# Attention with sinks: the rotation of keys and queries by block transfers instead of by products

## The reference, cut to what matters

```python
def apply_rope_2(x, cos, sin):
    x1, x2 = jnp.split(x.astype(jnp.float32), 2, axis=-1)
    return jnp.concatenate([x1 * cos - x2 * sin, x2 * cos + x1 * sin], axis=-1)

def swa_sink_mixer(h, positions, w_qkv, q_norm, k_norm, sinks, w_out):
    qkv = h @ w_qkv
    q, k, v = jnp.split(qkv, [1024, 1280], axis=-1)       # 16 heads, 4 heads, 4 heads of 64
    ...
    q = apply_rope_2(rms_norm_2(q, q_norm), cos, sin)
    k = apply_rope_2(rms_norm_2(k, k_norm), cos, sin)
    o = banded_sink_attention(q, k, v, sinks)
    return o.astype(h.dtype) @ w_out
```

## Time and profile before

| | |
|---|---|
| median of 3 runs | 2091.65 us (2090.82 to 2091.75) |
| the profiled execution | 2096.21 us, of which the span of the instructions is 2094.3 us |
| TensorE busy | 2067.1 us, 99% of the span |
| VectorE, ScalarE busy | 1779.1 us (85%), 1400.0 us (67%) |
| mean granted clock of TensorE | 0.995 of full |
| attention with sinks | from about 1771 us to 1850 us of the span |

### The profile page before, as it was taken

One profiled execution on the slowest core, in us unless ns is written; L12 is line 12 of the kernel. 1 busy time (PEld: TensorE's weight loads), 2 busy tenths in 40 slices (PEclk: granted clock), 3 DMA queues, 4 the chain that ended last, 5 costly groups with the idle time before them and its releaser, 6 DMA issues. The chain is left out here.

```text
span 2094.3 us, 27806 instructions
## 1 busy us (share of the span) xinstructions
PE 2067.1 (99%) x10830; PEld 1740.9 (83%) x10830; DVE 1779.1 (85%) x2358; ACT 1400.0 (67%) x1855; POOL 59.6 (3%) x58
## 2 busy tenths in 40 slices
PE   9999999999999999999999999999999999999999
PEld 8878888878888888888888888879988888778887
DVE  6776768789999999999999999988878888788887
ACT  5654547568888888888888888867745446565544
POOL 0011002001000000000000000000000000000000
PEclk9999999999999999999999999999999999999999
DMA  9537764659999999999999999954446555346552
GB/s 312 181 121 271 233 209 151 219 199 395 394 395 395 395 395 383 385 380 386 371 393 374 388 372 378 394 202 141 144 159 227 196 181 149 81 154 222 183 197 102
DMA packets 291275, 565.92 MB, mean 270 GB/s; under 512 B 13596, under 2 KB 120224, under 8 KB 290896
## 3 DMA queue, kind: packets, MB, share of 16 engines
q1 hardware_dynamic: 284480, 537.13, 71.8%
q0 software_dynamic: 5792, 23.78, 3.1%
q10 hardware_dynamic: 864, 3.15, 0.4%
HBM read 555.10 MB, written 12.59 MB: 271 GB/s over the span
## 5 line engine op out<-in xcount | busy, mean ns | idle before, releaser
L505 DVE TENSOR_TENSOR wl<-raw,wh 128x1024 fp32r<-128x1024 f32 x626 | 756.2, 1242 | 99.9 <-ACT wh L497 95.5
L497 ACT ACTIVATE wh<-raw 128x1024 fp32r<-128x1024 f32 x626 | 640.9, 1053 | 154.1 <-PE psum L542 61.7
L505 DVE TENSOR_TENSOR wl<-arena,wh 128x1024 fp32r<-128x1024 f32 x384 | 456.7, 1222 | 37.6 <-ACT wh L497 32.6
L497 ACT ACTIVATE wh<-arena 128x1024 fp32r<-128x1024 f32 x384 | 403.9, 1062 | 84.7 <-PE psum L542 82.5
L540 PE MATMUL psum<-wh,xhl 128*128 128x512 f32 (+1 forms) x1136 | 449.5, 396 | 1.8 <-DVE wl L505 0.9
L542 PE MATMUL psum<-wh,xhl 128*128 128x512 f32 (+1 forms) x1136 | 441.5, 389 | 0.0
L541 PE MATMUL psum<-wl,xhl 128*128 128x512 f32 (+1 forms) x1136 | 440.6, 388 | 0.0
L532 PE MATMUL psum<-xhl,wh 128*128 128x512 f32 x980 | 349.4, 396 | 0.0
L540 PE MATMUL psum<-wh,yh 128*128 128x512 f32 x752 | 295.6, 393 | 1.0 <-DVE yl L1714 1.0
L542 PE MATMUL psum<-wh,yl 128*128 128x512 f32 x752 | 293.0, 390 | 0.0
L541 PE MATMUL psum<-wl,yh 128*128 128x512 f32 x752 | 292.6, 389 | 0.0
(11 more groups left out here) (455 smaller groups left out, 2078.1 us busy)
## 6 DMA issues: line engine op xcount, KB each, us to landing
arena<-in_moe_g SPq DMA_DIRECT2D x72, 1024.0 KB, 8.8
arena<-in_moe_u SPq DMA_DIRECT2D x72, 1024.0 KB, 8.5
raw<-in_moe_d SPq DMA_DIRECT2D x64, 1024.0 KB, 8.8
arena<-in_moe_d SPq DMA_DIRECT2D x48, 1024.0 KB, 8.3
raw<-in_ff_up SPq DMA_DIRECT2D x48, 1024.0 KB, 5.2
raw<-in_moe_g SPq DMA_DIRECT2D x40, 1024.0 KB, 8.1
raw<-in_moe_u SPq DMA_DIRECT2D x40, 1024.0 KB, 9.2
raw<-in_ff_down SPq DMA_DIRECT2D x24, 1024.0 KB, 5.4
```

The costliest lines, as they stand in the source:

```text
L497: A.activation(unit_made(s, i)[0], raw_half(s, i), ACT.Copy).then_inc(*s.w_hi.tick(i))
L505: V.tensor_tensor(lo, raw_half(s, i), hi.bitcast(F), SUB).then_inc(*s.w_lo.tick(i))
```

## The change

For each pair of tiles the half-swap is no longer a product. Right behind `copied`, ScalarE waits for its own copy and then issues four transfers of 32 partitions x 512 values (64 KB each) that put block a of `T4` where block a^1 of `QB` stands. The gain, which was folded into `ROT`, becomes one column for each of queries and keys, `ROT_GAIN`: two products of the matrix with a gain vector (`rotated_gains`, at the head of `pe_window`) and a copy of 2 columns out of PSUM, in the place of two 128 x 128 multiplications on VectorE. `sines` waits for the transfers, one pair after the other, multiplies `T4` in place by gain and sine, and adds. `copied` of a later pair waits for the transfers of an earlier one and for its `sines` to be through with `T4`.

```diff
+    rotated = {(n, i): sig(f"rotated{n}{i}", 16) for n in range(3) for i in range(1 if n == 2 else 2)}
...
-    ROT = [SC[:, 640:768], SC[:, 768:896]]
+    ROT_GAIN = SC[:, 640:642]
...
-        def rope(n):
-            for i, b in enumerate(RO_BANKS[n]):
-                take(b)
-                T.wait_ge(*act.of(f"wi.qc{n}{i}"))
-                T.wait_ge(*dve.of("wi.rot"))
-                T.matmul(bk(b), ROT[n == 2], flat(QB[:, 2 * i:2 * i + 2, :]), start=True, stop=True
-                         ).then_inc(*pe.tick(f"wi.ro{n}"))
-                empties(b, (dve, f"wi.ro{n}"))
+        def rotated_gains():
+            ps = take(6)
+            for i, n in enumerate(("aqn", "akn")):
+                x = T.matmul(ps[:, i:i + 1], C("rot"), S(n), start=True, stop=True)
+            x.then_inc(*pe.tick("wi.rot"))
+            empties(6, (dve, "wi.rot"))
...
+        rotated_gains()
         project(2, 0, by_blocks("nm1"))
...
-        rope(2)
...
-        rope(0)
...
-        rope(1)
...
         def copied(n, i):
             A.wait_ge(*pe.of(f"wi.p{n}{i}"))
             if n != 2:
-                A.wait_ge(*pe.of(f"wi.ro{0 if n else 2}"))
+                A.wait_ge(*rotated[0 if n else 2, 0].of("all"))
                 A.wait_ge(*dve.of(f"wi.c0{i}" if n else "wi.c20"))
+                A.wait_ge(*dve.of(f"wi.q{0 if n else 2}"))
             A.activation(QB[:, 2 * i:2 * i + 2, :], heads(bk(Q_BANKS[n][i]), 2), ACT.Copy).then_inc(*act.tick(f"wi.qc{n}{i}"))
+            A.wait_ge(*act.of(f"wi.qc{n}{i}"))
+            for a in range(4):
+                A.dma_start(T4[32 * a:32 * a + 32, 2 * i:2 * i + 2, :], QB[32 * (a ^ 1):32 * (a ^ 1) + 32, 2 * i:2 * i + 2, :]
+                            ).then_inc(*rotated[n, i].tick("all"))
...
         def sines(n):
-            V.wait_ge(*pe.of(f"wi.ro{n}"))
+            V.wait_ge(*dve.of("wi.rot"))
             m = 2 * len(RO_BANKS[n])
-            for i, b in enumerate(RO_BANKS[n]):
-                V.tensor_tensor(T4[:, 2 * i:2 * i + 2, :], heads(bk(b), 2), CS[:, 1, :].unsqueeze(1).to_broadcast([P, 2, 256]), MUL
-                                ).then_inc(*dve.tick(f"wi.ro{n}"))
+            for i in range(len(RO_BANKS[n])):
+                V.wait_ge(*rotated[n, i].of("all"))
+                V.scalar_tensor_tensor(T4[:, 2 * i:2 * i + 2, :], T4[:, 2 * i:2 * i + 2, :], ROT_GAIN[:, (n == 2):(n == 2) + 1],
+                                       CS[:, 1, :].unsqueeze(1).to_broadcast([P, 2, 256]), MUL, MUL).then_inc(*dve.tick(f"wi.ro{n}"))
             V.wait_ge(*dve.last())
...
-        V.tensor_scalar(ROT[0], C("rot"), S("aqn"), None, MUL).then_inc(*dve.tick())
-        V.tensor_scalar(ROT[1], C("rot"), S("akn"), None, MUL).then_inc(*dve.tick("wi.rot"))
+        V.wait_ge(*pe.of("wi.rot"))
+        V.tensor_copy(ROT_GAIN, bk(6)[:, 0:2]).then_inc(*dve.tick("wi.rot"))
```

## The result

The changed kernel takes 2102.55 us (median of 5 runs, 2100.84 to 2104.15) against 2091.65 for the kernel before in the same comparison (2090.52 to 2093.1): a ratio of 1.0044 (95% interval 1.0032 to 1.0055), some 9 us lost where 1.4 were forecast as gained. It is outside the range. The quotient of these two medians alone would be 1.0052, 10.9 us; I go by the ratio on record and its interval.

What follows compares the result with a forecast made beforehand. TensorE, busy 99% of the span, bounds the kernel. Sums(0) 0.15 us early, logits(0,2) 0.4 late, weigh(0,0) 2.0 early and weigh(0,1) 1.4 early give 1.4 us off, 2091.65 to 2090.2; range 2086.5 to 2096.0.

Steps and rivals of the forecast that it cites:

- Up to sums(0): Head to sums(0): four issues of 0.44 us delay the square; sums(0) 0.15 us early, TensorE stands still 2.1 us.
- Rival two: Slower, chance 0.11: sines(0) waits for a 7.2 us landing, logits(0,2) waits 3.4 us, clock halves; +4.5 us, 2096.1.
- logits(0,2): Wait for q0: the transfer of (0,1) lands in 4.4 us, TensorE waits 0.6 us, logits start 0.4 us late.
- To weigh(0,0): Logits to weigh(0,0): ScalarE's copies and issues add 3.8 us; weigh(0,0) 2.0 us early, 5.2 us stay as a stall.
- To weigh(0,1): After weigh(0,0): landing 2.1 us, q1 lets logits(4,6) start 2.2 us early, half clock for 1.5 us; weigh(0,1) 1.4 us early.
- Rival three: Clearly faster, chance 0.11: issues cost ScalarE next to nothing, clock stays full, q1 at 1813.4; 6.9 us gained, 2084.8.

Runs made afterwards that it cites:

- e7: The changed kernel with the keys in buffers of their own, so copied(0,0) waits neither for the keys' landing nor their sines: 2098.04 us against 2094.12, ratio 1.0019.
- e2: The changed kernel with one 256 KB transfer behind each copy in place of four, the swap of partitions left out: 2093.21 us against 2093.74 for the kernel before.
- e3: The changed kernel with all 20 transfers issued from GpSimd's queue instead of ScalarE's: 2093.97 us against 2093.74 for the kernel before, ratio 1.0000.
- e12: The changed kernel with GpSimd issuing all transfers and the keys in buffers of their own: 2094.91 us against 2093.48 for the kernel before, ratio 1.0009.
- e6: The changed kernel with unread products on TensorE ahead of sums(0) and weigh(0,0), to hold the clock: 2100.59 us against 2094.12 for the kernel before, ratio 1.0036.
- e11: The changed kernel with the output weights' loads held until the transfers of the keys and of (0,1) have landed: 2101.21 us against 2093.48, ratio 1.0034.
- e1: The changed kernel with transfers going to an unused area and sines reading QB, so no product waits for a landing: 2101.6 us against 2093.74, ratio 1.0033.
- e4: The kernel before with only the late queries (1,0) and (1,1) rotated by transfers, rope(1) removed: 2094.24 us against 2093.74, ratio 1.0001.
- e5: The changed kernel with the square ahead of the four issues for (2,0), (0,0) and (0,1): 2103.37 us against 2094.12 for the kernel before, ratio 1.0051.
- e8: The kernel before, all products kept, with the 20 transfers issued from ScalarE into an unused area: 2105.78 us against 2094.12, ratio 1.0058.
- e9: The kernel before, without transfers, with squared(1,0) and squared(1,1) moved on ScalarE to right behind copied(1,1): 2090.33 us against 2093.48, ratio 0.9983.
- e10: The kernel before with only (1,0) and (1,1) rotated by transfers, rope(1) removed, the eight issues on GpSimd's queue: 2094.15 us against 2093.48, ratio 1.0002.

## Why the prediction was wrong

**"Up to sums(0)" is the step that failed**, in two terms. The first is a size: 0.44 us for an issue, 1.75 for four, from two transfers of another kind. Measured: 0.61, and 2.44 for four. That is past even the upper bound of 2.4 that I took from SP's issues, and those were the rows of the same order. The second is a judgement: "for the keys the same delay is harmless, since sums(2) comes 5 us behind its square". I followed the keys' square and not their buffer. copied(0,0) had waited for rope(2) and cosines to have read `QB`, and the last that it waited for was its own projection; now it waits until the keys have landed, and been rotated and added. In after they land 5 us after their issue, and copied(0,0) starts 3.9 us later than before (1782.97 is 4.07 behind the start of sums(2), against 0.20). So two sets of four issues stand in the chain to sums(0), where I had counted one. The stall before sums(0) became 4.53 us, not 2.1, with another 0.99 ahead of spread_keys, where the same landing holds VectorE. sums(0) is 3.8 us late behind sums(2); counted so, the forecast was 0.35 late (0.15 early, with sums(2) itself 0.5 early). e7 takes this one wait away and gets 5 us back, counted from after's ratio to e7's (1.0044 less 1.0019, and the intervals don't overlap); e2 and e3 take the issues away and get all 9 back, the wait still there. The wait without the issues costs nothing (e3 against e12), as ScalarE had 3.37 us of slack before copied(0,1); the issues without it cost 4 us (e7), both in a chain 9.

**The clock behind it.** Rival two had a half clock, but behind a wait of logits(0,2). It came one step sooner, behind the stall of sums(0), and makes the stretch to the logits 4.05 us longer (8.80 against 4.75). In after only about 1 us of that is its own: held up, it gives place to q0's wait (e6). Where q0 is early, the whole of it is (4.05 in e11, 3.1 in e1 and e7). Rival two asked for a stall longer than 2.4 us, and my expectation of e7 said that 2.3 would be too short. The runs show no such bound: the clock fell 2.4 us after TensorE stopped in the earlier trace rows, about 3.1 and 4.4 us after it stopped in after, and in e2 and e7 behind two stalls of at most 1.7 us each.

**"logits(0,2)": the landing was mis-sized, and the clock hid it.** I took 4.4 us for the transfer of (0,1), and 3.8 and 7.2 as the bounds; it was 6.7, so the row of the loads in the same stretch was the better neighbour, in spite of eight times fewer bytes. sines(0) waited 4.91 us, as rival two said it would, and q0 was there at 1799.8. But TensorE, at the half clock, reached logits only at 1801.11; at full clock it would have been there at 1797.1 and waited some 3 us. The Trainium skill, "DMA: Bandwidth & Descriptors", section "Queues, rings and completion order", would have had the small transfer take turns with the load; it does not land like one alone here, 6.7 us against 2.0 with the loads held (e11).

**"To weigh(0,0)": right in kind, short in size.** Forecast: all that stays of the stall and product is a stall of 5.2 us, 2.0 gained. Measured: 6.35, and 0.9 gained on the logits. From the start of copied(1,0) to soft(1) it is 3.09 us (1810.61 to 1813.70) instead of 0.48, and the same again behind copied(1,1): 5.2 us more of ScalarE, not 3.8. That is 1.4 of the 1.5 missing (2.0 and the 0.4 that the logits were to be late, less 0.9). e4 shows it alone: 33.35 against 34.11.

**"To weigh(0,1)": the landing was right, the clock not.** Landings of 2.1 us behind copied(1,1) came as taken. But behind the longer stall the clock was half through weigh(0,0) and logits(4,6) (2.08 us for the logits against 1.16 in the earlier trace rows), and again, behind the same wait of 0.78 as before, through weigh(0,1), which it hadn't been in the earlier trace rows. In e4, which has the early part of before and this late part, 0.76 gained at weigh(0,0) is a loss of 0.2 at weigh(0,1) and of 1.3 at the end. "Nothing behind weigh(0,1) changes" was wrong by that 1.1.

**The sum, as measured:** issues and the keys' wait 3.8, half clock 4.05, the late part -0.9 to weigh(0,0), then +1.0 and +1.1 for the half clock in logits(4,6) and behind weigh(0,1): 9.1 us. The nearest of my cases was rival two, in its sign and in its engine's clock, though not in place, at 0.11; its price, 4.5 us, was half of what was measured. I had let a gain of 1.4 us, the small remainder of large terms, name the forecast. Rival three (issues cost next to nothing) was measured by e2 and e3, where they nearly do: the gain of 6.9 us isn't there then either. weigh(0,0) does start 3.4 to 4.2 us sooner, but logits(4,6) follows at q1's pace, 1.9 to 2.8 sooner, with a half clock behind it, and the time ends at 1.000. The rival had q1 at 1813.4, 30.1 us behind sums(2), where it is there at 34.5 in e3, and left out VectorE's own list, which is full until then.

Open: why the clock fell again at the wait of 0.78 us before weigh(0,1) in after, e1, e4, e5, e6 and e7, and not in before or e8. In e9 and e10 it was half already, since sums(1).

## What to carry to other kernels

Cheap work that is moved to an engine's queue costs that engine its issue time each time: count the issues, take the longest similar issue in the trace, and see what stands behind them on that engine. When a product is replaced by a transfer, list not only who reads the result but who waits to overwrite the source, and price that with the landing beside whatever loads move then. And where TensorE, whose work is to be cut, stands still waiting for another engine, look at the order of that other engine's list before anything else: two lines moved gave about 3.5 us here (e9), and the twenty transfers, placed wherever they did no harm, gave nothing.

## What was unexpected of the hardware

- Four issues in a row of 64 KB from SBUF to SBUF hold ScalarE for 2.44 us, 0.61 each. The first row behind them also carries 2.52 us of idle time: what stands behind the issues starts when they are through. What stands ahead may still run: in e5 the issues begin at 1790.84, and the square ahead of them runs to 1791.30. One transfer of all 128 partitions took 0.47 us to issue, and on GpSimd one took 0.49. Two small issues of another kind had taken 0.38 and 0.45.
- A transfer of 64 KB lands in 1.9 to 2.1 us alone and in 4.4 to 7.0 beside loads of 512 KB; one of 256 KB takes 2.2 alone and 6.9 beside them (e2). Company counts here, size hardly.
- The same wait of 0.78 us left the clock at full in before (weigh(0,1) in 1.08 us) and at half in after (1.89). And stalls of 0.54 and 0.59 us, with only small products between them, were all the idle time ahead of a fall to half in e2.
